# The convolution group, its layer norm and the four recurrent heads in one block, with the projection tiles in a new order

## The chip, the cores and the metric

One core of a Trainium2 chip. The time is that of one execution of the whole program on the device, in microseconds (us); the median of three runs is 3102.73 us.

## What is computed

One layer over 1024 tokens of 1024 channels, all in fp32. The part in question:

```python
hn = _modulate(_rmsnorm(h, norm_mix_g), sh1, sc1)     # (1024, 1024)
q_r, ff_r, fb_r, i_r, g_r, c_a, c_g = jnp.split(hn @ w_in, splits, axis=-1)   # 7 groups of 512 channels
# convolution group
h = c_a * jax.nn.sigmoid(c_g)                         # gated pairs
h = depthwise_conv(h, w, width=31) + bias
hf = (h - mean(h)) * rsqrt(var(h) + EPS) * ln_g + ln_b   # over the 512 channels
o_c = silu(hf)
# recurrent group: 4 heads of 128, each forward and backward in chunks of 64
q = silu(q_r); v = i_r
k = (1 - lb) * sigmoid(-z); logf = log(lb + (1 - lb) * sigmoid(z))
b = cumsum(logf)                                      # within a chunk: the scan
qr = q * exp(b - b_mid); kr = k * exp(b_mid - b)      # the factors
ku = k * exp(b_last - b); qe = q * exp(b)
o = tril(qr kr^T) v + qe S                            # S: state before each chunk
o = o * rsqrt(mean(o * o) + EPS) * norm_g * silu(g_r)
mix = concat([o_h, o_c]) @ w_out
```

Then come the gate and residual, a second norm, the PEER retrieval (8 heads, top 16 of 128 x 128 experts) and a last norm with its own modulation. The modulation vectors are `silu(c) @ ada_w`.

## The kernel before

Six steps, each a block of five engine programs that ends with a barrier of all engines. Activations lie with channels on the 128 partitions and the 1024 tokens along the free dimension. `step1` makes the normed input `hn` as a pair of fp32r tensors, `hn_hi` and `hn_lo`, and projects the first gated pair. `step2` is the convolution, `step3` the four heads and the first part of the output projection, `step4` the rest of it and the second norm, `step5` the queries, `step6` the retrieval and the end.

**A projection tile** makes 128 of the 3584 columns of `hn @ w_in`, 28 tiles in all (`project`, L315). It is 48 matmuls of 128 x 512. Its weights come by DMA into `raw` (L300), ScalarE rounds them to `w_hi` (`round`, L305), GpSimd makes `w_lo` (`remainder`, L309), and the product goes to one of two PSUM slots, tile n to slot n % 2. So tile n needs the evacuation of tile n - 2, and its weights can be rounded only when tile n - 2 has been made.

**step2.** For each of four channel groups ScalarE takes the sigmoid of one tile into `sig` (L407), VectorE multiplies it by the other tile straight from PSUM (L548), and then makes 31 taps, one instruction each with a drain behind it (L550, L554). While it does, TensorE projects the next pair, and multiplies the 48 row blocks of the modulation weights, 8 slots of 512 KB (L392, L476). After that it projects head 0's `ff`, `fb` and `q`. After the last tap: means by matmul with ones (L509), subtraction (L558), squares (L445), variance (L527), a square root on ScalarE (L447), a reciprocal on VectorE (L561), the scaling (L564), silu and store (L451, L454). Head 0's `v` and the turning of the modulation rows into columns come last.

**step3.** On VectorE `prepare` (L934) makes the scans of a head and the differences for the exponents, ScalarE's `power` (L851) the exponentials, VectorE the four products with k and q per direction, the factors (L976 to L980). `recurrence` (L705) on TensorE turns v (L722) and ku (L727), makes the scores (L736), the products k v of the chunks (L749) and the output (L756 to L761). ScalarE copies the turned v to `vtok` (L897) and ku to `kt` (L904) before the next pair of PSUM banks is free; VectorE masks the scores (L990) and adds the states (L1002). Tiles of the next heads are projected in between, in the order `HEAD_TILES`. A head's norm is a sum by matmul with ones (L767), 1/P and eps on VectorE (L1022), a reciprocal on VectorE (L957), a square root on ScalarE (L864); then `finish` (L955) scales o.

All engines run their own instruction list in the order written; semaphores alone tie them together.

Of the kernel before, what the change touches and what calls it, by code (L numbers as in the profile page):

```python
# [30 lines left out]
HEAD_TILES = ([(x, 0) for x in ("ff", "fb", "q", "v")]  # L31
              + [t for h in range(HEADS - 2)
                 for t in (("ff", h + 1), ("fb", h + 1), ("q", h + 1), ("v", h + 1), ("g", h))]
              + [(x, HEADS - 1) for x in ("ff", "fb", "q")] + [("g", HEADS - 2), ("v", HEADS - 1), ("g", HEADS - 1)])
MADE = 4
# [84 lines left out]
def step1(nc, m, io, sem):  # L120
# [14 lines left out]
    with ctx:  # L135
# [12 lines left out]
        w_in, w_rounded = [sem(f"s1_w_in{s}") for s in range(2)], sem("s1_w_r")  # L148
        block = ctx.enter_context(nc.Block())

        @block.sync
        def _(sp):
# [6 lines left out]
            for n in range(2):  # L159
                sp.dma_start(raw[:, n, :], io["w_in"][n].rearrange("p k m -> p (k m)")).then_inc(w_in[n], 16)  # L160

# [167 lines left out]
def head_inputs(m):  # L329

    h, W = Mem(), 4 * KB
    h.low = [m.at(f"head_low{d}", [P, T], F32, F0 + W * d) for d in range(2)]
    h.kk = [m.at(f"head_k{d}", [P, T], F32, F0 + W * (2 + d)) for d in range(2)]
    h.q, h.vT = (m.at(f"head_{n}", [P, T], F32, F0 + W * k) for n, k in (("q", 4), ("vT", 5)))
    return h


def step2(nc, m, io, sem):
# [5 lines left out]
    A_SLOTS = 8  # L344
    A_PARTS = ((0, 2), (2, 5), (5, 8), (8, 16))
    head0 = m.head
    f = F0 + 28 * KB
    hp = at("s2_hp", [P, T + 2 * PAD], F32, f)
    acc = at("s2_acc", [P, CONV_C, T], F32, f + 5 * KB)
    work = at("s2_work", [P, T], F32, f + 21 * KB)  # L350
    r = at("s2_r", [P, T], F32, f + 26 * KB)
    sig = at("s2_sig", [P, T], F32, f + 38 * KB)
    e = R0 + 80 * KB
    ada = at("s2_ada", [P, A_SLOTS, D], F32, e)
    rows4 = at("s2_rows4", [P, D], F32, e + 32 * KB)
    rows2 = at("s2_rows2", [P, HALF], F32, e + 36 * KB)
    sq = [at(f"s2_sq{s}", [P, T], F32, (e + 44 * KB, f + 38 * KB)[s]) for s in range(2)]
    ctx = ExitStack()
    with ctx:
        w = Weights(m, sem, "s2w", raw_weights(m, "s2w", f + 30 * KB))  # L360
        ps = m.ps
        ps_mu = ctx.enter_context(nc.psum_tensor("s2_mu", [P, T], F32))
        ps_var = ctx.enter_context(nc.psum_tensor("s2_var", [P, T], F32))
        sig_ready, glu_done = sem("s2_sig_r"), sem("s2_glu")
        conv_done, mu_ready, d_ready, sq_ready, sq_used = (sem(f"s2_{n}") for n in ("conv", "mu", "d", "sqr", "squ"))
        var_ready, r_ready, xr, stored = (sem(f"s2_{n}") for n in ("var", "r_s", "xr", "out"))
        ada_in = [sem(f"s2_ada_in{s}") for s in range(A_SLOTS)]
        ada_used, mod_ready, zeroed = sem("s2_adau"), sem("s2_mod"), sem("s2_zeroed")
        row_ready, row_taken = sem("s2_row_r"), sem("s2_row_t")
        evac = sem("s2_evac")  # L370
        H0 = 2 * CONV_C

        def row_items(g):

            if g < DC:
                return [(4 * g + v, v, g) for v in range(4)]
            return [(2 * DC + 2 * g + v, 4 + v, g - DC) for v in range(2)]

        block = ctx.enter_context(nc.Block())

        @block.sync
        def _(sp):
            def load(c):
                for s in range(2):
                    w.load(sp, c, s, io["w_in"][c * 2 + s])

# [186 lines left out]


def step3(nc, m, io, sem):

# [1633 lines left out]
```

## Time and profile before

| what | us |
|---|---|
| median of three runs (lowest, highest) | 3102.73 (3090.29, 3103.9) |
| the profiled execution | 3088.44 |
| its span in the trace | 3086.6 |
| TensorE, VectorE, ScalarE, GpSimd busy | 2820.8, 2279.9, 836.8, 1253.5 |
| from the start to step2's first instruction | 77.5 |
| to the end of the last tap | 273.7 |
| to step3's first work | 308.8 |
| to the outputs of heads 0, 1, 2, 3 in PSUM | 397.5, 491.2, 577.7, 654.3 |
| to step4 | 680.2 |
| to step5 | 797.5 |
| steps 5 and 6, to the end | 3086.6 |

The page's slices are 77 us each, so slices 2 to 9 hold steps 2 and 3:

```
PE   6766989789889999899999999997999999999996
DVE  4997445641777999999999887865766767766777
ACT  3112434321211111475474675840000000000003
PEclk8888999789889999999999999998999999999998
```

Each digit is a busy share in tenths; PEclk is the clock granted to TensorE in tenths of full speed.

### The profile page before, as it was taken

The page shows a single profiled execution, that of the slowest core. Times are in us where ns is not written, and L with a number is a line of the kernel's source. Part 1 is how long each engine was busy: PE and PEld are TensorE (multiplying, and loading weights), DVE is VectorE, ACT ScalarE, POOL GpSimd, SP SyncE. Part 2 cuts the span into 40 slices and gives each one's busy share as a digit, 9 for nine tenths or more (in the row PEclk, how much of TensorE's full clock was granted, in tenths as well). Part 3 has the DMA queues.
Part 4 walks back from the last instruction along what each step waited for, and adds up shares of the span by engine and source line. Part 5 has one row for each costly group of instructions (what it writes and reads, how often), then busy time and mean ns, then how long its engine had stood idle before and what let it go on. Part 6 is the DMA issues. An engine that isn't in the chain of part 4 may idle for free.

```text
span 3086.6 us, 31337 instructions
## 1 busy us (share of the span) xinstructions
PE 2820.8 (91%) x10188; PEld 1542.5 (50%) x10188; DVE 2279.9 (74%) x4450; ACT 836.8 (27%) x1687; POOL 1253.5 (41%) x1103
## 2 busy tenths in 40 slices
PE   6766989789889999899999999997999999999996
PEld 3544777676675444454454454543444444444442
DVE  4997445641777999999999887865766767766777
ACT  3112434321211111475474675840000000000003
POOL 0111111021235544444444454444545655655652
PEclk8888999789889999999999999998999999999998
DMA  4540111023229999999999999999999999999995
GB/s 180 232 171 34 42 35 35 21 96 116 90 88 382 381 405 376 347 386 382 367 384 381 356 370 415 415 415 404 400 405 403 401 405 394 401 405 403 393 397 206
DMA packets 287037, 919.80 MB, mean 298 GB/s; under 512 B 26016, under 2 KB 75424, under 8 KB 279456
## 3 DMA queue, kind: packets, MB, share of 16 engines
q0 software_dynamic: 147456, 536.94, 44.5%
q1 hardware_dynamic: 100784, 301.75, 25.8%
q10 hardware_dynamic: 38640, 79.18, 6.6%
q8 instruction: 79, 1.29, 0.2%
q14 instruction: 78, 0.64, 0.1%
HBM read 830.21 MB, written 87.56 MB: 297 GB/s over the span
## 4 chain that ended last, share of the span: by engine, by line
PE 38%; DMA 16%; DVE 10%; POOL 2%; issue 2%; SPq 2%; ACT 1%; DVEq 0%; POOLq 0%
PE s_pu L1619 21%; DMA s_slot<-in_v,s_row 10%; DVE s_slot L2027 5%; DMA s_vt<-in_v_tiles 3%; PE s_pw L1656 3%; PE s_pw L1700 3%; PE s_pu L1700 3%; PE s_py L1700 3%; PE s_ph L1700 3%; POOL s_slot L1570 2%; PE s_py L1666 2%; DVE s_hB L2041 1%; DMA s_wr<-s_w 1%; SPq L1534 1%; SPq L1528 1%
## 5 line engine op out<-in xcount | busy, mean ns | idle before, releaser
L1619 PE MATMUL s_pu<-s_hn,s_ut 128*128 128x512 f32 x2304 | 1009.9, 595 | 0.0
L2041 DVE SCALAR_TENSOR_TENSOR s_hB<-s_slot,s_dot,s_hB 128x1024 f32<-128x1024 f32 x469 | 597.5, 1284 | 275.9 <-DMA s_slot<-in_v,s_row 273.6
L1570 POOL DMA_INDIRECT s_slot<-in_v,s_row x512 | 591.5, 1155 | 431.4 <-DVE s_hB L2041 334.0
L1570 POOL DMA_INDIRECT s_slot<-in_u,s_row x512 | 505.5, 987 | 588.1 <-DVE s_slot L2027 528.6
L1619 PEld LDWEIGHTS s_pu<-s_hn,s_ut 128*128 128x128 f32 x2304 | 434.8, 191 | 526.9 <-issue 526.9
L2027 DVE SCALAR_TENSOR_TENSOR s_slot<-s_slot,s_ph 128x1024 f32<-128x1024 f32 x512 | 608.6, 1220 | 88.8 <-DMA s_slot<-in_u,s_row 69.6
L1795 ACT ACTIVATE s_hotw<-s_hot,s_rest 128x128 bf16<-128x128 bf16 x1024 | 308.6, 423 | 27.7 <-ACT s_gst L1742 24.7
L1700 PE MATMUL s_pw<-s_ct,s_vt 128*128 128x512 f32 x512 | 248.6, 609 | 43.9 <-DMA s_vt<-in_v_tiles 43.9
L321 PE MATMUL s_ps<-hn_hi,w_hi 128*128 128x512 f32 x576 | 239.8, 416 | 40.5 <-POOL w_lo L309 12.4
L1852 ACT ACTIVATE s_sq<-y 128x512 f32<-128x512 f32 x16 | 8.9, 628 | 940.7 <-DVE y L2090 940.7
L1700 PE MATMUL s_pu<-s_ct,s_vt 128*128 128x512 f32 x512 | 243.7, 599 | 0.0
L1700 PE MATMUL s_py<-s_ct,s_vt 128*128 128x512 f32 x512 | 240.6, 592 | 0.0
L1700 PE MATMUL s_ph<-s_ct,s_vt 128*128 128x512 f32 x512 | 240.6, 592 | 0.0
L322 PE MATMUL s_ps<-hn_lo,w_hi 128*128 128x512 f32 x576 | 231.9, 403 | 0.0
L1742 ACT ACTIVATE s_gst<-s_pu 128x512 f32<-128x512 f32 x128 | 76.5, 598 | 466.6 <-PE s_pu L1619 466.4
L1700 PEld LDWEIGHTS s_pw<-s_ct,s_vt 128*128 128x128 f32 x512 | 98.5, 194 | 170.6 <-issue 143.4
L325 PE MATMUL s_ps<-hn_hi,w_lo 128*128 128x512 f32 x576 | 182.2, 398 | 0.0
L554 DVE SCALAR_TENSOR_TENSOR s_work<-s_hp,cols,s_work 128x1024 f32<-128x1024 f32 x116 | 170.5, 1470 | 8.7
L1700 PEld LDWEIGHTS s_pu<-s_ct,s_vt 128*128 128x128 f32 x512 | 99.4, 194 | 127.1 <-issue 127.1
L1700 PEld LDWEIGHTS s_py<-s_ct,s_vt 128*128 128x128 f32 x512 | 97.3, 190 | 122.5 <-issue 122.5
L1700 PEld LDWEIGHTS s_ph<-s_ct,s_vt 128*128 128x128 f32 x512 | 97.3, 190 | 122.5 <-issue 122.5
L309 POOL TENSOR_TENSOR w_lo<-s3w_raw,w_hi 128x1024 fp32r<-128x1024 f32 x16 | 37.8, 2364 | 296.6 <-ACT w_hi L305 296.6
(299 smaller groups left out, 3020.5 us busy)
## 6 DMA issues: line engine op xcount, KB each, us to landing
s_ut<-in_u_tiles SPq DMA_DIRECT2D x128, 512.0 KB, 7.3
s_vt<-in_v_tiles SPq DMA_DIRECT2D x32, 2048.0 KB, 20.8
s_g<-s_gst ACTq DMA_DIRECT2D x128, 256.0 KB
s_w<-s_wb ACTq DMA_DIRECT2D x16, 2048.0 KB, 11.8
s_gr<-s_g SPq DMA_DIRECT2D x64, 512.0 KB, 27.8
s_wr<-s_w SPq DMA_DIRECT2D x16, 2048.0 KB, 29.3
s_ada<-in_ada SPq DMA_DIRECT2D x48, 512.0 KB, 7.7
s_ada<-in_ada SPq DMA_DIRECT2D x4, 2048.0 KB, 20.4
```

What stands on the lines that cost most here:

```text
L321: pe.matmul(out[:, c], w_hi[:, k, :], x_hi[:, h, k, :], start=(k == first), stop=False)
L322: pe.matmul(out[:, c], w_hi[:, k, :], x_lo[:, h, k, :], start=False, stop=False)
L325: mm = pe.matmul(out[:, c], w_lo[:, k, :], x_hi[:, h, k, :], start=False, stop=(k == last))
L554: dve.scalar_tensor_tensor(dst, hp[:, k:k + T], cw[:, c, k:k + 1], work[:, :], ALU.mult, ALU.add)
L1570: pool.indirect_dma_start(out=slot[s][:, :], out_offset=None, in_=io[kind], in_offset=bass.IndirectOffsetOnAxis(ap=row[b][:, j:j + 1], axi ...
L1619: mm = pe.matmul(pu[:, n % 2, :], ut[n % UR][:, k, :], hn[:, k, :], start=(k == 0), stop=(k == DC - 1))
L1656: mm = pe.matmul(pw[:, unit % 2, j * P:(j + 1) * P], hot2[n % 2][:, q, :, t], hotw[n % 2][x][:, q, :, t], start=(x == 0), stop=(x == 2))
L1700: mm = pe.matmul(bank(c), vt[n // VG % VR][:, n % VG, c * P:(c + 1) * P], ct[:, n % CR, :], start=(n == 0), stop=(n == KEYS - 1))
L1742: act.activation(gst[n % 2][:, :], pu[:, n % 2, :], ACT.Gelu).then_inc(gelu_done, 1)
L1795: o = act.activation(hotw[n % 2][1 + x][:, q, :, t], hot1[n % 2][:, q, :, t], ACT.Copy, scale=rest[:, x, 8 * r + i:8 * r + i + 1])
L2027: dve.scalar_tensor_tensor(s, s, 1.0, ph[:, :], ALU.mult, ALU.mult, accum_out=dot[b][:, j:j + 1]).then_inc(taken, 1)
L2041: dve.scalar_tensor_tensor(y, s, dot[b][:, j:j + 1], y, ALU.mult, ALU.add).then_inc(taken, 1)
```

## The change

- `step2` and `step3` become one block, `front`. PSUM `s_mu` and `s_var` become `po` and `pv`, and the heads' two banks `pm` are the halves of `pv`. The scratch tensors of the convolution lie where the heads' states lie later.
- The 28 tiles stand in one list, `TILES`. `project_part`, `project_tiles` and the rounds walk through it. The gated halves of the pairs are copied out of PSUM by ScalarE into a buffer `abuf` (`linear`), so a pair can be made before VectorE wants it.
- The modulation rows come six per k (one buffer of 3 MB) behind tiles 2 to 9, each set loaded when the set before has been used; the first two weight loads of the block are issued in `step1`.
- On VectorE head 0's scans stand after the third channel group, its factors after the tenth tap of the fourth. Head 1's `ff`, `fb`, `q`, `v`, head 0's `g` and head 2's `q` are projected before the last tap's means; `q` has two buffers, head 1's `v` waits in `o`. Head 2's `ff` is projected inside head 0's products in place of `g`.
- Each square root and reciprocal (convolution norm, heads 0 to 3, step 4, step 6; not step 1) becomes `Ln` and then `Exp` with scale -0.5 on ScalarE. In the heads it reads the sums in PSUM itself.
- The states of head 0 start from a memset that waits until the convolution's stores have landed.

The core of the diff:

```diff
+TILES = [("sig", 0), ("glu", 0), ("sig", 1), ("glu", 1), ("ff", 0), ("fb", 0), ("sig", 2), ("glu", 2),
+         ("q", 0), ("v", 0), ("sig", 3), ("glu", 3), ("q", 1), ("v", 1), ("ff", 1), ("fb", 1),
+         ("g", 0), ("q", 2), ("ff", 2), ("fb", 2), ("v", 2), ("g", 1), ("ff", 3), ("fb", 3),
+         ("q", 3), ("g", 2), ("v", 3), ("g", 3)]
+EARLY_TAPS = 10
```

On the queue of SyncE:

```diff
+            for n in range(2, NT):
+                k = n - ADA_AT
+                if 0 <= k < DC:
+                    if k:
+                        sp.wait_ge(ada_used, k)
+                    for s in range(6):
+                        sp.dma_start(ada[:, s, :], io["ada"][2 + s][:, k, :]).then_inc(ada_in[s], 16)
+                src = io["w_in"][n + 2] if n + 2 < NT else io["w_out"][n + 2 - NT]
+                w.load(sp, (n + 2) // 2, n % 2, src)
+            sp.wait_ge(conv_stored, 16 * CONV_C)
```

On GpSimd, after the remainders of tiles 2 to 19:

```diff
+            pool.wait_ge(conv_done, CONV_C)
...
+            pool.drain().then_inc(st_zero, 1)
+            pool.wait_ge(conv_stored, 16 * CONV_C)
+            for d in range(2):
                 pool.memset(state[d][:, 0, :], 0.0)
+            pool.drain().then_inc(state_zero, 1)
```

On TensorE:

```diff
+            for n in range(2, 16):
+                project_part(n, range(DC))
+                if 0 <= n - ADA_AT < DC:
+                    ada_rows(n - ADA_AT)
...
+                if n == ADA_AT + DC:
+                    columns()
+            pe.wait_ge(mod_taken, 1)
+            means(range(CONV_C - 1))
+            project_tiles(("g", 0), ("q", 2))
+            means((CONV_C - 1,))
...
+            recurrence(0)
+            project_tiles(("fb", 2))
+            sums(0)
+            recurrence(1)
+            project_tiles(("ff", 3))
+            sums(1)
+            project_tiles(("fb", 3), ("q", 3))
+            recurrence(2)
+            project_tiles(("v", 3))
+            sums(2)
+            recurrence(3)
```

On ScalarE, from the rounding of tile 15 on:

```diff
+            power(0, 0)
+            power(0, 1)
+            act.wait_ge(w.used, tile_of("fb", 1) + 3)
+            for n in (16, 17):
+                round_tile(n)
+            forget(1, 0)
+            forget(1, 1)
+            gate(0)
+            round_tile(18)
+            query(2)
+            round_tile(19)
+            conv_norm()
...
             for h in range(HEADS):
                 nxt = h + 1 < HEADS
+                if h and nxt:
+                    for d in range(2):
+                        forget(h + 1, d)
+                        round_tile(tile_of(("ff", "fb")[d], h + 1) + 2)
+                    if h > 1:
+                        query(h + 1)
...
+                keys_turned(h)
...
+                if not h:
+                    conv_out()
+                    kept_value()
...
+                root_of(h)
...
             def root_of(h):
-                act.wait_ge(inv, h + 1)
-                act.activation(r[:, :], r[:, :], ACT.Sqrt)
...
+                if h:
+                    act.wait_ge(done, h)
                 for b in range(2):
...
+                    act.wait_ge(pm_ready[b], 9 * h + 9)
+                    act.activation(r[:, b * HALF:(b + 1) * HALF], pm[b], ACT.Ln, scale=1.0 / P,
+                                   bias=m.eps[:, 0:1]).then_inc(pm_used[b], 1)
+                act.drain()
+                act.activation(r[:, :], r[:, :], ACT.Exp, scale=-0.5)
```

On VectorE:

```diff
+            for c in range(CONV_C - 1):
+                gated(c)
+                taps(c, range(CONV_W))
+            dve.wait_ge(reset_ready, 1)
+            dve.wait_ge(ada_used, DC)
             prepare(0)
+            gated(CONV_C - 1)
+            modulation()
+            taps(CONV_C - 1, range(EARLY_TAPS))
+            scale(0)
+            taps(CONV_C - 1, range(EARLY_TAPS, CONV_W))
+            dve.wait_ge(mu_ready, 1)
```

## Rows read from the trace of the kernel before

**Rows 1.** Stages: stretch, length, busy PE PEld DVE ACT POOL, clock, DMA, GB/s

```profile
77.50:273.70 196.20, 135.60 (x636) 89.04 (x636) 185.70 (x132) 24.51 (x24) 31.32 (x11) 0.87 0.42 161
273.70:308.80 35.10, 24.82 (x80) 15.02 (x80) 16.33 (x14) 14.86 (x13) 2.39 (x2) 0.79 0.15 60
308.80:397.50 88.70, 82.87 (x553) 69.35 (x554) 35.65 (x62) 36.50 (x37) 15.30 (x11) 0.93 0.13 42
397.50:491.20 93.70, 84.94 (x558) 70.50 (x558) 46.55 (x68) 36.13 (x37) 11.83 (x5) 0.93 0.11 34
491.20:577.70 86.50, 77.10 (x510) 64.40 (x510) 46.53 (x68) 34.05 (x35) 9.40 (x4) 0.88 0.10 31
577.70:654.30 76.60, 56.32 (x421) 47.48 (x420) 56.02 (x71) 28.33 (x31) 12.29 (x5) 0.78 0.15 56
```

**Rows 2.** What TensorE waited for from 75 to 690 us; total, times, longest

```profile
PE s_pm L727 <- ACTq L906: 26.8, 4, 14.8
PE s_mu L476 <- DMA s_ada<-in_ada: 26.1, 4, 12.2
```

**Rows 3.** VectorE's timeline, convolution; start, duration, line, operation

```profile
79.88 1.23 DVE L548 TENSOR_TENSOR s_hp<-s_ps,s_sig 128x1024 f32<-128x1024 f32 x1
272.34 1.28 DVE L554 SCALAR_TENSOR_TENSOR s_acc<-s_hp,cols,s_work 128x1024 f32<-128x1024 f32 x1
277.52 4.62 DVE L558 SCALAR_TENSOR_TENSOR s_acc<-s_mu,s_acc 128x1024 f32<-128x1024 f32 x4 [3.90 <-PE s_mu L509]
289.68 6.55 DVE L561 RECIPROCAL s_r<-s_r 128x1024 f32<-128x1024 f32 x1 [7.54 <-ACT s_r L447]
```

**Rows 4.** Taps' line, remainders' line; count: shortest, median, longest ns

```profile
L554 DVE SCALAR_TENSOR_TENSOR s_work<-s_hp,cols,s_work x116: 1283/1285/3299, 82.1 to 271.0; 128x1024 f32<-128x1024 f32 x116
L309 POOL TENSOR_TENSOR w_lo<-s2w_raw,w_hi x12: 2342/2616/3448, 82.7 to 305.5; 128x1024 fp32r<-128x1024 f32 x12
```

**Rows 5.** A projection, eight modulation rows; busy PE PEld DVE ACT, clock, DMA

```profile
397.37:408.54 11.17, 11.16 (x48) 8.90 (x48) 0.00 (x0) 0.00 (x0) 1.00 0.00 1
153.70:157.32 3.62, 3.61 (x32) 0.72 (x32) 0.00 (x0) 0.00 (x0) 1.00 0.17 36
```

**Rows 6.** Landing of modulation loads; of the convolution's stores (median us)

```profile
DMA to landing us min/median/max: 3.5/7.7/11.1
s_mix<-s_acc ACTq DMA_DIRECT2D x4, 512.0 KB, 2.6
```

**Rows 7.** ScalarE's timeline, logarithms of head 0 and what follows

```profile
310.32 2.59 ACT L881 ACTIVATE head_low<-head_low,lb,omlb 128x1024 f32<-128x1024 f32 x2
312.99 1.28 ACT L854 ACT_TABLE_LOAD   x1
```

**Rows 8.** VectorE's timeline, head 0's states to head 1's factors

```profile
370.23 2.66 DVE L1002 SCALAR_TENSOR_TENSOR s_state<-s_state,s_dec,s_pm 128x128 f32<-128x128 f32 x8 [11.30 <-PE s_pm L749]
397.59 1.23 DVE L1016 COPY s_o<-s_po 128x1024 f32<-128x1024 f32 x1 [11.56 <-PE s_po L761]
410.32 1.50 DVE L1022 TENSOR_SCALAR s_r<-s_pm 128x512 f32<-128x512 f32 x2
421.52 6.55 DVE L957 RECIPROCAL s_r<-s_r 128x1024 f32<-128x1024 f32 x1
```

**Rows 9.** ScalarE in order of time, heads 1 and 3

```profile
416.75 1.28 ACT L815 ACT_TABLE_LOAD   x1 [2.27 <-DVEq L981]
424.77 1.28 ACT L826 ACT_TABLE_LOAD   x1
437.23 1.01 ACT L897 ACTIVATE s_vtok<-s_po 128x1024 f32<-128x1024 f32 x1
609.64 1.06 ACT L864 ACTIVATE s_r<-s_r 128x1024 f32<-128x1024 f32 x1 [11.81 <-DVEq L958]
```

**Rows 10.** Timelines: VectorE in step 4's norm, ScalarE at the end

```profile
768.00 6.55 DVE L1126 RECIPROCAL s_r<-s_r 128x1024 f32<-128x1024 f32 x1 [4.36 <-ACT s_r L1075]
3072.24 10.66 ACT L1875 ACTIVATE y<-y,mods 128x512 f32<-128x512 f32 x16 [4.25 <-DVE y L2110]
```

More of the change, by code:

```diff
@@ L160, in _ @@
                 sp.dma_start(raw[:, n, :], io["w_in"][n].rearrange("p k m -> p (k m)")).then_inc(w_in[n], 16)
+            sp.wait_ge(row_ready, 1)
+            for s in range(2):
+                sp.dma_start(m.front_raw[s][:, :, :], io["w_in"][2 + s]).then_inc(ahead, 16)
+            sp.wait_ge(ahead, 32)
         @block.scalar
@@ L585, in step3, with front @@
+def front(nc, m, io, sem):
+    at, col = m.at, m.col
+    hd = m.head
     W = 4 * KB
     f = [F0 + n * W for n in range(18)]
-    low, kk, q, vT = m.head.low, m.head.kk, m.head.q, m.head.vT
-    vtok = at("s3_vtok", [P, NB, P], F32, f[7])
-    qe = [at(f"s3_qe{d}", [P, T], F32, f[8 + 4 * d]) for d in range(2)]
-    ku = [at(f"s3_ku{d}", [P, T], F32, f[9 + 4 * d]) for d in range(2)]
-    qr = [at(f"s3_qr{d}", [P, T], F32, f[10 + 4 * d]) for d in range(2)]
-    kr = [at(f"s3_kr{d}", [P, T], F32, f[11 + 4 * d]) for d in range(2)]
@@ new lines, in _ @@
+            sigmoid(0)
+            round_tile(3)
+            sigmoid(1)
+            round_tile(4)
+            linear(1)
+            round_tile(5)
+            forget(0, 0)
+            round_tile(6)
+            forget(0, 1)
+            round_tile(7)
+            logs(0)
+            sigmoid(2)
+            round_tile(8)
+            linear(2)
+            round_tile(9)
+            query(0)
+            round_tile(10)
+            value(0)
+            round_tile(11)
+            take_rows()
@@ new lines, in _ @@
+            sigmoid(3)
+            round_tile(12)
+            linear(3)
+            round_tile(13)
+            query(1)
+            round_tile(14)
+            keep_value()
+            round_tile(15)
+            power(0, 0)
[9 more added lines that the diff above has]
+            round_tile(19)
@@ L950, in prepare @@
[L950 to L963 removed]
+                    scan_of(m, dve, d, h).then_inc(prep[d], 1)
@@ new lines, in gated, with taps @@
+            def gated(c):
+                dve.wait_ge(sig_ready, c + 1)
+                if c:
+                    dve.wait_ge(a_ready, c)
+                src = abuf if c else ps[1]
+                dve.tensor_tensor(hp[:, PAD:PAD + T], src[:, :], sig[:, :], ALU.mult).then_inc(glu_done, 1)
+                dve.drain()
+            def taps(c, ks):
+                for k in ks:
+                    if k == 0:
+                        dve.tensor_scalar(work[:, :], hp[:, 0:T], cw[:, c, 0:1], bias[:, c:c + 1], ALU.mult, ALU.add)
+                    else:
+                        dst = work[:, :] if k < CONV_W - 1 else acc[:, c, :]
+                        dve.scalar_tensor_tensor(dst, hp[:, k:k + T], cw[:, c, k:k + 1], work[:, :], ALU.mult, ALU.add)
+                    done_now = dve.drain()
+                if CONV_W - 1 in ks:
+                    done_now.then_inc(conv_done, 1)
```

585 lines of the change are left out of this document (234 added, 351 removed).

## The prediction

> **What bounds the kernel now.** I read the slices first, then the busy times by stage, then the waits, and last the timelines of single engines. The chain of waits is of no use here: its pieces begin at 906 us. Steps 5 and 6 (from 797.5 us) are as they were but for the roots at the end; every step begins behind a barrier of all engines, so what the front saves or loses is passed on whole.
>
> Steps 2 and 3 take 602.7 us, 77.5 to 680.2. The reader is to see that the limit changes from stage to stage [rows 1]. Until the last tap VectorE is busy 185.7 of 196.2 us and TensorE only 135.6. Then, for 35.1 us (norm of the convolution, head 0's v, barrier), no engine is full. In heads 0 and 1 TensorE is at 83 of 89 and 85 of 94; in head 3 it is at 56 of 77, and it waits there up to 14.8 us for ScalarE's copies [rows 2]. So work of TensorE moved into the taps is free, and what VectorE does between the last tap and head 0's outputs is not.
>
> **The tap phase.** Before, the first gated pair is multiplied at 79.88 and the last tap ends at 273.6 [rows 3], 193.7 us. A tap takes 1.285 us, the longest 3.3; the long ones are those beside which GpSimd starts a remainder, 2.6 us long [rows 4]. Eleven remainders fall into the stage [rows 1]; each costs VectorE some 1.95, together 21.4, and leaves 172.3 for the four groups alone. After the change:
> - Start: rounding (1.06), table load (1.28) and sigmoid (1.0) from 77.6 give 81.0.
> - The four groups: 172.3.
> - prepare(0) moves here. Head 1's ran from the end of the copy of o at 398.8 to 410.3 with 0.5 idle, so 10.9 [rows 8]. The factors: from the end of the row at 410.32 (411.8) to the reciprocal at 421.52 [rows 8], 9.5. The modulation's small sums: 0.8.
> - Remainders: tiles 3 to 19 are split in this phase, 17 instead of 11: 17 x 1.95 = 33.2.
>
> Sum 307.7, 34 later than the last tap now.
>
> **Is TensorE there in time?** A projection takes 11.17 and eight modulation rows 3.62, so six rows 2.7, both at granted clock 1.00 [rows 5]. Tile 2 starts at 81.3 and, partly at half clock after the pause, ends near 96; then tiles 3 to 9 and the rows cost 13.9 each, tile 10 and the columns 12.8, tiles 11 to 15 11.2 each: tile 13 at 243 and tile 15 at 265. Each set of six loads is issued when the set before is used. The first of a burst lands after 3.5, the last of eight after 11.1 [rows 6]; six are there after some 9.9, inside the 11.2 of the projection. power(0) stands behind the rounding of tile 15, that is behind tile 13: done by 255, and VectorE asks for it at about 262. Head 1's sigmoids wait for factors(0) near 271, `g` and `q` of tiles 16 and 17 follow until about 299. So all of it is covered by VectorE's 307.7; if TensorE were more than some 8 us late, this cover would be gone.
>
> **From the last tap to head 0's output.** Means, subtraction, squares and variance stay: from 273.6 to the reciprocal at 289.68, 16.1 [rows 3], so 323.8 with the `Ln` in the place of the square root. The reciprocal (6.55) goes; a table load of 1.28 and an `Exp` of 1.06 come: 326.2. That a load stands between the two rests on head 0's logarithms, which end at 312.9 and have a load at 312.99 before the exponentials [rows 7]. The Trainium skill ("ScalarE: Activation LUTs", "Table sets: the hidden batching unit") says that one set holds both exp and ln, so that ln and then exp need one load. Here the trace shows two.
>
> Then ScalarE copies vtok and the four pieces of kt, 4.5 by the same work at 437 to 444: 330.8. The stores of the convolution stand behind that: silu's load 1.28, four times 1.69 for silu and issue, landing 2.6 [rows 6], GpSimd's memset and drain 0.7: 342. The head's states may not start before. That is a new wait; queued behind it on VectorE are the states of all parts, and TensorE's products behind them. From the first state to the copy of o takes 370.23 to 397.59, 27.4 [rows 8]. So o is copied at 369.2, against 397.6: **28.4 saved**. Barrier, scans and factors account for it; a tile's worth of `v` (11.7) has also left the head.
>
> **Head 1.** Times from the copy of o; before, 93.7 to the next [rows 1]. ScalarE ends power(1) at 16.9 (2.27 before the load at 416.75 [rows 9]). root_of(0) stands next: load, two `Ln` (1.4), load, `Exp`, 5.1, until 22.0; then head 2's two sigmoid pairs and roundings, the 8.0 between the two loads at 416.75 and 424.77 [rows 9], until 30. vtok begins there, before at 437.23 - 397.59 = 39.6. Behind it the square root and its load (2.4) no longer stand. In between TensorE has only `fb` to do and idles. **12.0 saved.**
>
> **Head 2.** It keeps its three tiles ahead. root_of(1) now precedes the sigmoids, so `q`'s weights are rounded 3.0 later; 2.4 come back behind vtok. **0.6 lost.**
>
> **Head 3.** Before, ScalarE took vtok, loaded the table and sat 11.81 until VectorE's reciprocal behind the factors, and began the square root at 609.64 [rows 9]; kt came after it at 610.8. Now loads, `Ln`, `Exp` and vtok run from 595.4 without VectorE: kt begins at 601.6. **9.2 saved.** After this head TensorE is full until 677.8, nothing more there.
>
> **Step 4 and the end.** In step 4 the reciprocal of 6.55 at 768.00 [rows 10] is on the path; load and `Exp` take 2.4: **4.1 saved**. At the end two reciprocals of 3.35 go, but ScalarE takes the last 16 pieces in 10.66 from 3072.24 [rows 10], and with square root, squares and the four new instructions it is free for them at 3072.1: nothing.
>
> Sum 28.4 + 12.0 - 0.6 + 9.2 + 4.1 = 53.1 us. Against the profiled execution's own 3088.44 that is 3035; the median of the runs lies 14.3 above that execution, and gives 3102.7 - 53.1 = 3049.6. I forecast 3050.
>
> **Bounds of what the trace doesn't show.**
> - The wait for the stores (4 us or so over what the scores need): 0, if the masked scores are the later ones, to 8.
> - The remainders beside the taps: 1.95 each by the rows; 0 for those that fall beside nothing, 2.6, the whole remainder, at most. Six more make 0 to 16; I take 11.7.
> - The clock in the pauses of heads 0 and 1: a tile behind a pause took 13.4 instead of 11.2; up to 9 more per head at half clock. I take what the heads show now, and keep 0 to 15.
> - Unrolled instruction lists of SyncE and GpSimd instead of loops: 0 to 3; neither engine is late anywhere.
>
> **Rivals.**
> - *The heads keep their pace.* Heads 1 and 3 have waits under the ones removed (banks freed by ScalarE, masking, low clock), and only the first 28 and the 4 count. For: TensorE's waits for `pm` are spread over four heads [rows 2]. Against: head 3's 11.81 is plainly VectorE's. Time 3102.7 - 32 = 3070. Chance 0.17.
> - *Root without its second load.* If `Ln` and `Exp` shared a table, 1.28 would go at the convolution's norm, in heads 1 to 3 and in step 4, 6.4 together: 3043. This is what the Trainium skill's rule named above would make of it. Against it stand rows 7. Chance 0.06.
> - *TensorE becomes the bound of the tap phase.* One buffer for six loads puts a DMA wait between every two tiles. Now such waits add up to 26.1 in four times [rows 2], and the granted clock of this stage is 0.87 [rows 1]. If every set is late by 3 us and the clock stays at its lower level (1.2 instead of 2.4 GHz), a tile with its rows takes 22.3 + 5.4 + 3 = 31, tiles 2 to 15 about 8 x 31 + 6 x 22.3 = 382: power(0) comes near 420 and the last tap at 455 instead of 307.7. That is 147 less 53 slower, 3197. It decides from the point where tile 13 ends later than some 250 (243 forecast); up to about 60 us of delay there the whole would still be no slower. Against: the loads fit by 1.3 us. Chance 0.04 for slower than before.
> - *The convolution doesn't overlap as written*, because some order among ScalarE's waits (sigmoid, linear, forget) holds a tile back by a whole group of taps: the front saves only the barrier and reciprocals, about 12, 3090. Chance 0.05.
>
> The forecast itself has 0.68. Its own range is 3035 to 3065; 3027 to 3077 takes in the clock's and the remainders' bounds, the first rival, and that the runs before lie 14 us apart. What a measurement of this kernel can tell from no change is 0.5%, 15.5 us: faster means under 3087. Faster 0.92, within 0.04, slower 0.04.
>
> **What would show it.** Last tap at about 308 with 17 long taps; no idle time on VectorE before factors(0); TensorE idle some 8 us before the last means; the first state of head 0 ended by GpSimd's memset near 342; copies of o at 369, 451, 538 and 605; a load between each `Ln` and `Exp`; step 4's root to its first scaling 2.4 instead of 6.6; the last 16 pieces unmoved from the end. Wrong would be: modulation loads as TensorE's largest wait, a clock near 0.6 before 265, vtok in head 1 later than 38 after the copy of o.

## The result, and the profile after

The changed kernel takes 3055.92 us (median of 4 runs, 3044.34 to 3058.29) against 3102.28 of the kernel before on the same chip: ratio 0.986, 95% interval 0.983 to 0.989. It was timed twice more beside other kernels: 3038.41 against 3088.51 (0.984, 0.983 to 0.986) and 3049.91 against 3096.91 (0.984, 0.982 to 0.987). So 46 to 50 us are gained; 53 were forecast, and 3050 us for the whole.

The profiled execution of the changed kernel took 3044.34, its span 3042.6. Its stages, cut at the last tap, the first state and the heads' copies of o, answer to [rows 1]:

```profile
core 0: us, PE busy (x) PEld busy (x) DVE busy (x) ACT busy (x) POOL busy (x), PEclk, DMA share, GB/s
75.00:310.80 235.80, 211.79 (x990) 155.90 (x988) 219.71 (x152) 63.88 (x62) 51.57 (x20) 0.95 0.40 148
310.80:345.90 35.10, 27.26 (x196) 17.37 (x197) 15.15 (x25) 22.18 (x22) 2.19 (x4) 0.65 0.15 61
373.30:451.50 78.20, 60.75 (x461) 50.91 (x461) 38.58 (x65) 35.17 (x37) 9.45 (x4) 0.89 0.11 34
539.20:606.70 67.50, 55.43 (x421) 46.56 (x421) 48.57 (x69) 30.87 (x34) 12.34 (x5) 0.85 0.18 64
```

In the taps VectorE is now busy for 219.7 us and TensorE for 211.8, where it was 135.6: the work that moved in is covered. The norm, from VectorE's timeline (start, duration, in brackets the idle time before and what ended it), answers to [rows 3] and [rows 8]:

```profile
309.47 1.28 DVE L936 SCALAR_TENSOR_TENSOR s_acc<-s_hp,cols,s_work 128x1024 f32<-128x1024 f32 x1
314.68 4.62 DVE L978 SCALAR_TENSOR_TENSOR s_acc<-s_po,s_acc 128x1024 f32<-128x1024 f32 x4 [3.92 <-PEq L636]
329.33 4.63 DVE L982 TENSOR_TENSOR s_acc<-s_acc,s_r 128x1024 f32<-128x1024 f32 x4 [10.04 <-ACT s_r L804]
334.17 6.41 DVE L994 COPY_PREDICATED s_st<-mask,s_pv 32x256 f32<-32x256 int32 x16 [0.21 <-PE s_pv L584]
345.89 1.29 DVE L1008 SCALAR_TENSOR_TENSOR s_state<-s_state,dec,s_pv 128x128 f32<-128x128 f32 x4 [5.32 <-POOLq L492]
```

The last row shows the wait that the change added: head 0's first state stands behind GpSimd's memset, and that behind the convolution's stores. ScalarE's timeline shows the root with a table load between its two functions, as [rows 7] had it:

```profile
325.76 1.11 ACT L802 ACTIVATE s_r<-s_pv,eps 128x1024 f32<-128x1024 f32 x1 [1.06 <-PEq L643]
326.95 1.28 ACT L804 ACT_TABLE_LOAD   x1
328.24 1.06 ACT L804 ACTIVATE s_r<-s_r 128x1024 f32<-128x1024 f32 x1
```

All profiles of this study, cut at the same points, in us between them. "Taps" runs from the first gated pair to the end of the last tap; c0 to c3 are the starts of the copies of the heads' outputs; s5 is step 5's first copy of a query on ScalarE; res is the first residual of step 6. Ratios are to the kernel before, timed beside each.

| kernel | taps | to c0 | c0-c1 | c1-c2 | c2-c3 | c3-s5 | s5-res | rest | ratio (95%) |
|---|---|---|---|---|---|---|---|---|---|
| before | 193.7 | 124.0 | 93.7 | 86.5 | 76.6 | 143.5 | 2244.1 | 44.7 | |
| before_again | 193.4 | 125.4 | 95.1 | 86.4 | 76.6 | 143.5 | 2244.1 | 44.7 | 1.000 (0.999-1.001) |
| after | 229.1 | 62.5 | 78.3 | 87.6 | 67.5 | 139.2 | 2250.4 | 46.3 | 0.986 (0.983-0.989) |
| after_again | 229.1 | 60.7 | 80.7 | 86.9 | 66.9 | 138.8 | 2242.5 | 46.8 | 0.984 (0.983-0.986) |
| after_five | 228.7 | 62.3 | 80.8 | 87.0 | 66.9 | 138.9 | 2260.9 | 47.6 | 0.984 (0.982-0.987) |
| roots_by_sqrt | 228.9 | 65.5 | 78.1 | 83.4 | 73.0 | 143.2 | 2244.1 | 46.2 | 0.986 (0.984-0.987) |
| factors_late | 199.6 | 105.6 | 78.3 | 87.5 | 67.5 | 139.2 | 2242.6 | 47.0 | 0.989 (0.987-0.990) |
| remainders_twice | 260.0 | 63.0 | 79.7 | 87.7 | 67.5 | 139.3 | 2241.1 | 47.4 | 0.994 (0.992-0.996) |
| remainders_on_vector | 217.4 | 62.1 | 79.8 | 86.3 | 66.6 | 138.9 | 2254.0 | 47.6 | 0.982 (0.979-0.985) |
| keys_first | 228.9 | 61.2 | 76.2 | 87.3 | 67.0 | 138.9 | 2244.1 | 47.4 | 0.984 (0.981-0.986) |
| stores_first | 229.1 | 60.3 | 81.0 | 87.1 | 67.0 | 138.8 | 2256.1 | 47.0 | 0.984 (0.981-0.987) |
| all_edits | 217.8 | 61.7 | 81.4 | 85.1 | 67.4 | 139.5 | 2242.6 | 47.0 | 0.978 (0.976-0.979) |
| combination_a | 217.2 | 62.6 | 73.5 | 83.9 | 66.7 | 139.2 | 2254.2 | 47.3 | 0.978 (0.975-0.981) |
| combination_b | 217.0 | 62.5 | 72.6 | 94.2 | 67.7 | 139.9 | 2262.6 | 47.2 | 0.981 (0.979-0.984) |

In three profiles of the changed kernel the columns up to s5 repeat within 1.8 us, head 1's (c0-c1) within 2.6. Head 1's scatter is TensorE's: for the same matmuls it is busy 60.8 us at granted clock 0.89 in the first of them, 63.6 at 0.85 in the second. The column s5-res, where no instruction differs, lies anywhere from 2241 to 2263; what a run has there above 2245 is called its slip below. So an edit of a few us is judged here by its own column, and the whole only where the edit is larger.

### The profile page after: what moved, and what is told of

Read it like the earlier page. It is cut to its first block, busy times and chain, and to the rows that moved or that the text cites. A ratio compares the mean times of both kernels' runs of the same rounds, so it can differ in the third digit from the quotient of the medians.

```text
span 3042.6 us, 31244 instructions
## 1 busy us (share of the span) xinstructions
PE 2822.3 (93%) x10188; PEld 1546.2 (51%) x10188; DVE 2242.5 (74%) x4436; ACT 861.7 (28%) x1712; POOL 1240.5 (41%) x1103
## 4 chain that ended last, share of the span: by engine, by line
DMA 23%; PE 19%; DVE 18%; POOL 5%; issue 3%; SPq 1%; ACT 1%; another core or an unknown queue 1%; DVEq 1%; ACTq 0%
DMA s_slot<-in_v,s_row 21%; PE s_pu L1623 15%; DVE s_slot L2033 9%; POOL s_slot L1574 5%; DVE s_hB L2047 2%; PE s_pw L1660 2%; PE s_py L1670 1%; DMA s_wr<-s_w 1%; SPq L1538 1%; DMA s_slot<-in_u,s_row 1%; DVE pk_key L1296 1%; DVE pk_key L1287 0%; DVE pk_rep L1288 0%; DVE s_eq L1942 0%
## 5 line engine op out<-in xcount | busy, mean ns | idle before, releaser
L1574 POOL DMA_INDIRECT s_slot<-in_v,s_row x512 | 577.8, 1128 | 451.9 <-DVE s_hB L2047 355.9
L330 PE MATMUL s_ps<-hn_hi,w_hi 128*128 128x512 f32 x576 | 239.7, 416 | 33.2 <-POOL w_lo L318 17.0
L318 POOL TENSOR_TENSOR w_lo<-s2w_raw,w_hi 128x1024 fp32r<-128x1024 f32 x28 | 73.7, 2635 | 436.1 <-ACT w_hi L314 436.1
```

The costliest lines, as they stand in the source:

```text
L318: pool.tensor_tensor(self.lo[s][:, :, :], self.raw[s][:, :, :], self.hi[s][:, :, :].bitcast(F32), ALU.subtract).then_inc(self.split, 1)
L330: pe.matmul(out[:, c], w_hi[:, k, :], x_hi[:, h, k, :], start=(k == first), stop=False)
L1574: pool.indirect_dma_start(out=slot[s][:, :], out_offset=None, in_=io[kind], in_offset=bass.IndirectOffsetOnAxis(ap=row[b][:, j:j + 1], axi ...
```

## Experiments

**Two controls.** The changed kernel again:

> The changed kernel once more, unchanged, to see how far two profiled executions of one kernel differ by stage. In the profile of the changed kernel the front up to the last head's copy took 606.7 us and step 5 began at 745.9, 52.0 us earlier than before; the whole gained only 46 to 48. If the missing part is scatter of the first product loop of step 6 (one pause of 9 us between its 1500th and 2000th matmul), the front is again within 1 us of 606.7 and the stretch from the start of step 5 to the first residual falls anywhere between 2244 and 2251 us. If the change costs something there (the rival), that stretch is again at 2250, 6 us above the kernel before.

It was 2242.5, so the change doesn't cost the 6 us every time, and the rival falls as it was put. Whether slips are more frequent with the change is not shown: both profiles of the kernel before have 2244.1, but its executions scatter too, beside after_five from 3088.15 to 3107.54. Two bounds were missed by 1.5 us: the stretch was expected at 2244 or more, and the front within 1 us of 606.7, where it took 605.2. The later run beside the combinations shows how large a slip can be:

> The changed kernel unchanged, beside the two combinations on the same chip: ratio to the kernel before 0.984 to 0.986; last tap 229 us after the first gated pair, copies of the heads' outputs 80.7, 87 and 67 us apart.

Ratio 0.984 and 228.7, 80.8, 87.0, 66.9, as expected; s5-res, of which nothing was said, was 2260.9. Stretches of its first product loop (time, then busy us and count of each engine, granted clock, DMA share, GB/s), first of after_again, then of after_five, with the same matmuls in each:

```profile
1653.90:1761.60 107.70, 107.13 (x458) 54.32 (x456) 97.47 (x285) 76.05 (x200) 45.83 (x45) 1.00 0.96 361
1761.60:2047.20 285.60, 285.60 (x1125) 141.98 (x1123) 215.53 (x348) 171.25 (x440) 144.92 (x146) 1.00 1.02 406
```

```profile
1657.80:1765.50 107.70, 107.13 (x458) 54.32 (x456) 97.78 (x288) 76.02 (x200) 46.56 (x46) 1.00 0.97 365
1765.50:2067.90 302.40, 291.55 (x1125) 143.52 (x1123) 217.76 (x351) 171.31 (x440) 144.97 (x147) 0.98 0.99 386
```

The first stretch is alike to 0.01 us on TensorE; in the second it stands still for 10.9 us and works 6 us longer, with a dip of the clock. What starts such a pause stays open: the waits name the engine's own issue and one copy of ScalarE. The kernel before:

> The kernel before, unchanged, to see its own scatter by stage. In its first profile step 5 began at 797.8, steps 5 and 6 took 2244.1 up to the first residual, and the rest 44.7; in six profiles of the changed kernel and its variants the rest took 46.2 to 47.6, also with the old roots. If that rest is scatter, it is 45 to 48 here; if it belongs to the change, though no instruction of it differs with the old roots, it is 44.7 again. The front is expected within 2 us of 797.8, and the ratio to the kernel before within 0.3% of 1.

Ratio 1.000, s5-res again 2244.1, and the rest 44.7, not 45 to 48. So the rest is not scatter: every kernel with the new front has 1.5 to 2.9 more there. This is taken up below. Step 5 began at 800.1, 2.3 later than in the first profile and just outside the 2 us expected, so what the front gained is known to about 2 us.

**The roots as before**, all seven, the rest of the change kept:

```diff
-                act.activation(r[:, :], pv[:, :], ACT.Ln, scale=1.0 / DCONV, ...)
-                act.drain()
-                act.activation(r[:, :], r[:, :], ACT.Exp, scale=-0.5).then_inc(conv_root, 1)
+                act.activation(r[:, :], pv[:, :], ACT.Sqrt, scale=1.0 / DCONV, ...)
+                act.drain().then_inc(conv_root, 1)
             dve.wait_ge(conv_root, 1)
+            dve.reciprocal(r[:, :], r[:, :])
+            dve.drain()
```

> The changed kernel with all seven roots made as before (square root on ScalarE, reciprocal of 6.55 us on VectorE) and everything else kept. Theory (a root costs only what is late at its place): the first rescaling of the convolution about 4 us later than 329.3, the power of head 1 and 2 earlier because ScalarE has 5 us less to do before it (2.3 us gained each), head 3 about 6 us later, step 4 about 4 us later, the tail some 1.7 us shorter: in all +8 to +10 us, ratio to the changed kernel about 1.003. Rival (the predicted attribution, roots worth what the working gave them): +14 to +17. Rival (each reciprocal stands on the path in full, 7 times 6.55 less what Exp and its table load cost): +25.

Measured: 3044.20 against 3038.41 of after_again on the same chip, 5.8 slower, under the 8 to 10 of the theory; by the columns, against after_again, +4.8 in the norm, -2.6 and -3.5 in heads 1 and 2, +6.1 in head 3, +4.4 in step 4, -0.6 at the end: 8.6 together, and 8.0 against the first profile of the changed kernel. The theory holds by the columns and is nearest for the whole; the other two fall. The signs are the lesson: in heads 1 and 2 ScalarE is late, and there a second table load and an `Exp` (2.4 us) cost more than a reciprocal on VectorE. Head 2's 3.5 are clear of its scatter. Head 1's 2.6 are not (against the first profile they are 0.2), but its landmark is: the copy of the turned v begins 27.2 us after the copy of o, and 29.3 after it in each of the three profiles of the changed kernel. With the old root, and with the new one in after_again:

```profile
403.24 1.00 ACT L784 ACTIVATE s_vtok<-s_po 128x1024 f32<-128x1024 f32 x1
```

```profile
399.98 1.01 ACT L786 ACTIVATE s_vtok<-s_po 128x1024 f32<-128x1024 f32 x1
```

(c0 is 376.0 there and 370.7 here.) In head 3 VectorE is late; TensorE's waits from 537.5 to 610 say so (us in total, times, longest), with the old roots 10.3 us for the masked scores, on which the reciprocal of 561.57 to 568.12 stands:

```profile
PE s_pv L584 <- DVEq L997: 10.3, 2, 9.5
```

and 1.8 in after_again. So of the 50 us that this chip shows between the kernels, the roots are 6 (8 by the columns), and 44 are everything else. What of these is the barrier between the two blocks that is gone, and what the moved tiles, no run separates; the next one separates the order on VectorE.

**Head 0's factors after the taps:**

```diff
-            prepare(0)
             gated(CONV_C - 1)
             modulation()
-            taps(CONV_C - 1, range(EARLY_TAPS))
-            scale(0)
-            taps(CONV_C - 1, range(EARLY_TAPS, CONV_W))
+            taps(CONV_C - 1, range(CONV_W))
+            prepare(0)
+            scale(0)
```

> The changed kernel with head 0's scans and factors after the convolution's last tap, as they were before the change, the rest kept. Theory (moving them between the taps hides ScalarE's powers and the tiles that wait on them): the last tap ends near 285 instead of 310.8, the factors are then made in the open, with two waits for ScalarE's exponentials, and the last tiles g and q come after them, so that the first subtraction of the mean starts near 340 instead of 314.7: +25 us on the whole. Rival (VectorE is the bound and only its sum of work counts, 29.4 us wherever it stands): first subtraction at 312 to 318, whole within 3 us.

13.1 us slower than after_again (15.3 at the start of step 5), so order counts, but little more than half of what the theory gave. The last tap ended at 281.2, and the first subtraction came at 327.9, not at 340. VectorE's scans and factors took 24.9 with no wait worth naming, because the exponentials of one direction ran under the scans of the other; the cost is TensorE's, which stood 33.9 us until ScalarE had freed a bank behind the powers, and then had two tiles left:

```profile
PE s_ps L330 <- ACTq L703: 33.9, 1, 33.9
```

```profile
327.87 4.62 DVE L977 SCALAR_TENSOR_TENSOR s_acc<-s_po,s_acc 128x1024 f32<-128x1024 f32 x4 [21.80 <-PEq L636]
```

**The price of a remainder.** Twice, and then on VectorE:

```diff
             for n in range(4, 20):
+                pool.wait_ge(w.rounded, n + 1)
+                pool.tensor_tensor(w.lo[n % 2][:, :, :], w.raw[n % 2][:, :, :], w.hi[n % 2][:, :, :].bitcast(F32),
+                                   ALU.subtract)
+                pool.drain()
                 w.remainder(pool, n // 2, n % 2)
```

> The changed kernel with each remainder of weight tiles 4 to 19 (GpSimd's subtraction of 2.35 to 2.6 us) made twice, same values. Theory (each such subtraction costs VectorE's two-input instruction beside it about 1.95 us, whichever it is, and VectorE bounds the taps' stretch): 16 more stretched instructions, last tap 31 us later (near 342), whole about +31. Rival (GpSimd's work beside VectorE is free, the long taps have another cause): last tap at 311, 0. Rival (VectorE stands still for GpSimd's whole instruction): +40. If TensorE's wait for the tiles' low parts decides instead, the tiles come later by 2.4 us each, and the wait of VectorE at the gated pairs shows it.

30.9 more in the taps and 30.5 in the whole, for 16 subtractions, 1.9 us each, as the theory had it; both rivals fall. The middle taps of the changed kernel, and then of this one (count, busy us, mean ns):

```profile
L936 DVE SCALAR_TENSOR_TENSOR s_work<-s_hp,cols,s_work 128x1024 f32<-128x1024 f32 x116 | 170.7, 1472 | 9.1 <-issue 0.4
```

```profile
L940 DVE SCALAR_TENSOR_TENSOR s_work<-s_hp,cols,s_work 128x1024 f32<-128x1024 f32 x116 | 208.3, 1796 | 9.1 <-issue 0.4
```

Over all instructions of VectorE in the taps, those above the shortest of their own line and operation add up to 35.4 us, nearly all in 17 long ones (the changed kernel, 17 remainders), and 66.3 in 33 (this one, 33 remainders): a mean of 2.1 and 2.0. Single ones lie between 1.9 and 2.2, whichever instruction the remainder meets, but for one: a multiplication that takes 0.81 elsewhere takes 3.76 beside the first remainder. The Trainium skill ("SBUF — State Buffer", "SBUF: two separate sides") has VectorE and GpSimd share a pair of ports that one holds "for the whole instruction; the other fully blocks"; that rule stood behind the +40, and the runs bear out that there is one such stop for each subtraction, shorter than its 2.35. The trace shows the wait on GpSimd's side too. A subtraction that starts while a tap runs lasts up to 3.46 instead of 2.35, and ends 2.1 to 2.2 us after the next tap has begun, however long it lasted; in the changed kernel, for instance, it runs from 98.22 for 3.04, and the long tap starts at 99.09.

```diff
+REM_AT = {(0, 10): 4, (0, 19): 5, (0, 29): 6, (1, 6): 7, (1, 15): 8, (1, 24): 9, ...}
-            for n in range(4, 20):
+            pool.wait_ge(w.split, 18)
+            for n in range(16, 20):
                 w.remainder(pool, n // 2, n % 2)
...
                 for k in ks:
+                    if (c, k) in REM_AT:
+                        ...
+                        w.remainder(dve, n // 2, n % 2)
```

> The changed kernel with the remainders of weight tiles 4 to 15 made by VectorE itself, between two taps shortly after each tile is rounded; GpSimd keeps tiles 2, 3 and 16 to 19. Theory (a remainder on GpSimd costs VectorE's instruction beside it 1.97 us, on VectorE it costs its own 1.22 and a gap): 12 times 0.66 less, last tap 8 us earlier (310.0 to 302), whole 7 to 8 us faster. Rival (the long taps have another cause, rounding on ScalarE or the arriving loads, and stay long): 12 times 1.3 more, last tap at 325. Rival (TensorE sets the pace once VectorE is faster): last tap at 306 to 310, with a wait of VectorE before the fourth gated pair or before the factors.

Taps 11.7 shorter, not 8; the two rivals fall. Now:

```profile
L943 DVE SCALAR_TENSOR_TENSOR s_work<-s_hp,cols,s_work 128x1024 f32<-128x1024 f32 x116 | 156.7, 1351 | 8.3 <-issue 0.4
L319 DVE TENSOR_TENSOR w_lo<-s2w_raw,w_hi 128x1024 fp32r<-128x1024 f32 x12 | 14.7, 1225 | 0.9
```

5 long ones are left with 9.9 us of the 35.2 that the 17 had, so 25.3 went (2.11 each where the expectation had 1.97) and 14.7 came. The time between the instructions (the stage less the sum of their durations) fell by 0.9, where the expectation had added some. That makes 11.5 of the 11.7. VectorE had no wait before the fourth pair or the factors, so TensorE is not yet the bound. Step 5 began at 733.0, 11 to 13 us earlier than in the changed kernel; the whole, with a slip of 10 in s5-res, doesn't tell it from the changed kernel: 0.982 (0.979 to 0.985) against 0.984.

**Copies of keys before the sigmoids in head 1:**

```diff
+                if h == 1:
+                    keys_turned(h)
                 if h and nxt:
                     for d in range(2):
                         forget(h + 1, d)
...
-                keys_turned(h)
+                if h != 1:
+                    keys_turned(h)
```

> The changed kernel, where in head 1 ScalarE copies the turned values and keys (vtok, kt) before head 2's two pairs of sigmoids and their roundings instead of after them. Theory (these 7.5 us on ScalarE keep TensorE from head 1's scores and from the tile v behind them): tile v starts near 403.5 instead of 409.1, head 1 from copy to copy 5 us shorter (80.7 to about 75.5), whole -5. Rival (tile v needs the bank that the sigmoids free and the weights rounded behind them, so it comes no earlier): -1 to +1, with TensorE waiting for w_lo or for the bank.

Head 1 in 76.2 against 80.7 of after_again, so 4.5, and below all the profiles of the changed kernel, as the theory had it; the whole, 0.984, can't show it. TensorE's waits in head 1 (total, times, longest), in after_again from 365 to 455 us, and now from 370 to 447:

```profile
PE s_pv L575 <- ACTq L793: 10.5, 1, 10.5
```

```profile
PE s_pv L575 <- ACTq L793: 2.9, 1, 2.9
PE s_ps L330 <- POOL w_lo L318: 2.4, 1, 2.4
```

Tile `v` now starts at 403.97, after a wait of 2.4 for its low part, which the rival named: it is the next limit there, not an equal one.

**Stores in another order:**

```diff
-                for c in range(CONV_C):
-                    act.wait_ge(xr, c + 1)
+                for i, c in enumerate((0, 2, 1, 3)):
+                    act.wait_ge(xr, i + 1)
...
-            pool.wait_ge(conv_stored, 16 * CONV_C)
+            pool.wait_ge(first_stored, 32)
```

> The changed kernel with the convolution's four blocks scaled and stored in the order 0, 2, 1, 3; GpSimd clears the first states after two stores, and VectorE waits for the other two before the second part of the states. Theory from the trace of the changed kernel (TensorE's quarter of a tile after the first products runs 5.2 us at the lower clock and ends only 0.5 us before the second products are let go by the states): the first state starts 2.7 us earlier, after the first products, but the copy of head 0's output comes only about 0.5 us earlier, whole within 1 us. Rival (the wait for the stores is on the path in full, as the prediction counted it): first state 5 us earlier, and the copy with it, whole -4 to -5.

The first state came at 341.19, 2.1 earlier than in after_again, released by TensorE and no longer by GpSimd; the second group of states came at 348.04 and the copy at 370.82, where after_again has 347.91 and 370.71. From the first scaling of the norm, which came 0.5 later in this run, the copy is 0.4 earlier (43.2 against 43.6), which is the theory's 0.5:

```profile
341.19 2.66 DVE L1012 SCALAR_TENSOR_TENSOR s_state<-s_state,dec,s_pv 128x128 f32<-128x128 f32 x8 [2.30 <-PE s_pv L600]
348.04 2.66 DVE L1012 SCALAR_TENSOR_TENSOR s_state<-s_state,dec,s_pv 128x128 f32<-128x128 f32 x8 [4.19 <-PE s_pv L600]
```

So the wait of 5 us was worth 0.4: TensorE has a quarter of a tile to do behind the first products, which takes 5.2 us at 0.63 us a matmul (0.39 a few us later), and only then asks for what the states release.

**All together, and two combinations.**

> The three edits before together, and two more: head 0's keys are multiplied by their constant on ScalarE instead of VectorE, and the roots of heads 0 and 1 (not those of 2 and 3, of the convolution and of step 4) are square root and reciprocal again. If the parts add: taps -8, constant -1.5 to -3, head 1 -5, roots of heads 0 and 1 by the traces -2.6 and -3.5, stores 0: about -20 against the changed kernel, ratio to it 0.993. If TensorE takes over as the bound in the taps or in head 1 (its sum there is 83 of 94 us before the change), -10.

3024.63, 0.978 (0.976 to 0.979), the first that is clearly faster than the changed kernel (0.984, 0.982 to 0.987, on the same chip). But the whole flatters it: of the 30.2 us between its profiled execution and that of after_five, 11.3 lie in the front and 18.3 are after_five's slip. The ratio of the two wholes, 0.993, is the expected one, but by the front the -20 was missed and something near the -10 came, and not because TensorE took over. The taps kept their 11, head 2 its 2; head 1 lost its 5, because the reciprocal and two stretched products of VectorE stood ahead of the masks, and TensorE waited 12.5 us for these. VectorE's rows, and TensorE's waits for the masks from 75 to 690 us (total, times, longest):

```profile
383.43 6.55 DVE L971 RECIPROCAL s_r<-s_r 128x1024 f32<-128x1024 f32 x1
390.06 3.17 DVE L974 TENSOR_TENSOR head_o<-head_o,s_r 128x1024 f32<-128x1024 f32 x1
393.32 3.20 DVE L977 SCALAR_TENSOR_TENSOR head_o<-head_o,cols,s_g 128x1024 f32<-128x1024 f32 x1
396.63 6.40 DVE L1013 COPY_PREDICATED s_st<-mask,s_pv 32x256 f32<-32x256 int32 x16
```

```profile
PE s_pv L588 <- DVEq L1015: 17.7, 8, 12.5
```

Combination a leaves out the new order of the stores and moves head 0's rescaling:

```diff
                 if h:
                     scale(h)
-                    finish(h - 1)
+                    if h not in (1,):
+                        finish(h - 1)
...
+                if h in (1,):
+                    finish(h - 1)
                 for part in range(4):
```

> The changed kernel with: remainders of tiles 4 to 15 and the constant of head 0's keys as in the run with all edits (stores in the old order); head 1's copies of values and keys before head 2's sigmoids; roots of heads 0 and 1 by square root and reciprocal; and head 0's rescaling, with its reciprocal, after head 1's masked scores instead of before. In the run with all edits VectorE reached the masks 12.5 us late because the reciprocal of 6.55 and two stretched products stood ahead of them. Theory: without that, tile v in head 1 starts as soon as its low part is there, 31 us after the copy, and head 1 takes 73 to 74 us from copy to copy (80.7 in the changed kernel, 81.4 with all edits); head 2 85. The whole 20 to 24 us faster than the changed kernel, ratio to it 0.993. Rival (moved behind the masks, the rescaling makes the states or head 0's store late): head 1 at 77 or more.

Head 1 took 73.5, as expected, head 2 83.9, and step 5 began at 724.0, 22.1 before after_five's. The whole: 3029.41 against 3049.91, 20.5 faster. It is the fastest front; its ratio to the kernel before, 0.978, is that of all_edits, since its s5-res had a slip of 10.

Combination b has `(1, 2)` in place of `(1,)` in both conditions.

> As combination a, with head 1's rescaling, too, after head 2's masked scores. Theory (in head 2 TensorE waits under 1 us for the masks, so nothing is won, and ScalarE, which waits for the rescaled output before head 3's logarithms, comes later): 0 to 1 us slower than combination a. Rival (the reciprocal of 6.55 delays the masks there too): head 2 at 83 instead of 85, 2 us faster.

Both expectations fell: head 2 took 94.2, 10.3 more, and the whole 3038.35, 8.9 more. VectorE, combination a first:

```profile
480.71 6.42 DVE L1012 COPY_PREDICATED s_st<-mask,s_pv 32x256 f32<-32x256 int32 x16 [14.22 <-PE s_pv L586]
489.38 2.66 DVE L1028 SCALAR_TENSOR_TENSOR s_state<-s_state,dec,s_pv 128x128 f32<-128x128 f32 x8 [2.26 <-PE s_pv L600]
```

```profile
480.64 6.40 DVE L1012 COPY_PREDICATED s_st<-mask,s_pv 32x256 f32<-32x256 int32 x16 [25.18 <-PE s_pv L586]
487.15 6.55 DVE L969 RECIPROCAL s_r<-s_r 128x1024 f32<-128x1024 f32 x1
496.57 2.64 DVE L1028 SCALAR_TENSOR_TENSOR s_state<-s_state,dec,s_pv 128x128 f32<-128x128 f32 x8 [0.19 <-issue]
```

Before the masks VectorE had sat idle for 14 us even after the rescaling; behind them it is due within 2.3. The same move wins in head 1, where tile `v` stands between masks and states. Here it loses 8.1: the first state starts 63.3 us after the copy of o instead of 55.2. The rest is on TensorE, which is busy 81.4 us instead of 75.5 with the same matmuls, at granted clock 0.84 instead of 0.92.

## Why the prediction came near, point by point

- **Tap phase.** 307.7 forecast, 310.75 measured. Of the three us 0.7 are the start (81.68), the rest the price of a remainder: 17 long instructions as counted, 35.4 us instead of 33.2, and remainders_twice and remainders_on_vector show that the remainders are their cause. TensorE was there in time: tile 13 ended at 242.1 and tile 15 at 263.9 (243 and 265 forecast), VectorE had no wait before the factors (asked for at 264.2), and TensorE waited 0.7 in all for modulation rows, where the rival wanted 3 per tile. The granted clock was 0.95. With that two rivals fall, TensorE as the bound and taps that don't overlap.
- **Norm and root.** 18.5 forecast from last tap to first scaling, 18.6 measured, 17.1 and 18.4 in the two later profiles. The load at 326.95 settles the rival without it: the rule of the Trainium skill ("ScalarE: Activation LUTs", "Table sets: the hidden batching unit"), by which `Ln` and then `Exp` need one load, does not hold for this program.
- **The wait for the stores.** The place was right (GpSimd's memset ends it, 345.9 against 342), its weight was not: the prediction put it at 4 us over what the scores need, and stores_first shows that it was worth 0.4. The 4 us were due to TensorE all the same, so that the sum came out is luck.
- **Copy of o in head 0.** 28.4 saved by forecast; 24.3 in the first profile, 26.9 in the second. The 4.1 missing in the first are mostly the late last tap (3.1) and the stretch from the norm to the first state (0.8); from the first state to the copy it took the 27.4 forecast.
- **Heads 1 to 3.** 12.0, -0.6 and 9.2 forecast; 15.4, -1.2 and 9.1 in the first profile, 13.0, -0.5 and 9.7 in the second. The mechanism was right as well: counted from the copy of o, ScalarE's copy of the turned v began at 29.3 in head 1 (30 forecast, 39.6 before), and the copies of kt in head 3 at 23.9 (23.9 forecast, 33.0 before). What head 1 gains in the first profile over the second (15.4 against 13.0) is luck: TensorE was busy 60.8 us there instead of 63.6 for the same matmuls, at granted clock 0.89 instead of 0.85. Rival one, that the heads keep their pace, falls.
- **Step 4.** 4.1 forecast, 4.3 to 4.7.
- **To the start of step 5.** 53.1 forecast in all; 52.0, 53.8 and 51.8 measured against the first profile of before.
- **At the end: nothing, said the prediction. That step failed.** It asked when ScalarE would be free, not what the longer root does to TensorE behind it. ScalarE's squares of the other half stand behind that root and start 2.0 later, so TensorE waits 3.37 instead of 1.39, and does the 16 matmuls of the last sums more slowly. The same stretch in the kernel before, with the old roots, in after_again and in after_five:

```profile
3060.20:3067.30 7.10, 7.07 (x16) 2.89 (x16) 3.07 (x1) 3.46 (x7) 0.00 (x0) 1.00 0.01 2
```

```profile
3017.40:3024.60 7.20, 7.11 (x16) 2.96 (x16) 3.13 (x1) 3.54 (x8) 0.00 (x0) 1.00 0.01 2
```

```profile
3007.60:3016.40 8.80, 8.76 (x16) 3.55 (x16) 4.75 (x8) 4.76 (x8) 0.00 (x0) 0.81 0.01 2
```

```profile
3027.40:3037.60 10.20, 10.16 (x16) 4.04 (x16) 4.74 (x8) 4.77 (x9) 0.00 (x0) 0.70 0.01 2
```

  The eleven profiles with the new root all have the pause of 3.37, and there the 16 matmuls take 8.6 to 10.2 us at a granted clock of 0.70 to 0.82; the three with the old roots have 1.39, 7.1 and 1.00. So 2.0 are lost by the longer pause and 1.5 to 3.1 by the slower matmuls, and the new root saves 2.4 on its own way (2.57 from the second `Ln` to the last 16 pieces, 4.93 with the old roots): 1.1 to 2.7 lost where nothing was forecast. What else the new kernels have over the kernel before, like the 1.5 of roots_by_sqrt, lies in the transposes ahead (there its granted clock is 0.84 against 0.94); nothing of the change is near them, and why they differ stays open.
- **"Passed on whole."** Every column up to s5 was passed on, but the 2241 to 2263 of unchanged code behind it are not a constant. In the profiled execution of the changed kernel they took 6.3 us more than in that of the kernel before. Together with the end (1.6) this is the difference between 52.0 at step 5 and 44.0 in the two spans.

## What to carry to other kernels

Before an exchange of one function for two on another engine is made everywhere, ask at each place which engine is late there: here the same exchange gained 6 us in head 3, and lost 3.5 in head 2 and about 2 in head 1. Idle time of an engine can be used only where it lies: a rescaling of 9 us was free between masks and states in one head and cost 10 in the next, and the column to look at is what stands between the two on TensorE. And after a large change that moves stages, read again what each engine does first after its longest wait: in head 1 ScalarE did 7.5 us of work for the next head before the copies that TensorE stood 10.5 us for. Cut every trace at the same landmarks, and see how far the unchanged stages scatter, before an edit of a few us is believed.

## What the runs showed of the hardware

- A subtraction of two fp32 tiles of 128x1024 on GpSimd (2.35 to 3.5 us) stretches one instruction of VectorE that it meets: 17 of 17 and 33 of 33 times, by 2.1 and 2.0 us in the mean (1.9 to 2.2, once 3.0). Made on VectorE it takes 1.22.
- Between `Ln` and `Exp` stood a table load of 1.28 us in the norm, in the heads, in step 4 and at the end.
- TensorE's 16 matmuls of the last sums took 7.1 us at granted clock 1.00 after a pause of 1.4 us (three profiles), and 8.6 to 10.2 at 0.82 to 0.70 after a pause of 3.4 (eleven).
- Code that no edit touched took 2241 to 2263 us. From the 1400th to the 2000th of the 2304 matmuls of the first product loop it was 321.8 to 322.5 in eight profiles, and 331 to 344 in the six that took 2250 or more.
